# Hymba step with a mixture of experts: expert blocks of 130 to 150 rows by rank of count, and a router with stacked weights

## Chip, cores and metric

One core of one Trainium2 chip. The metric is the device time of one execution in microseconds; the time before is 1022.97 us, the median of 3 runs (1019.84 to 1026.25).

## What is computed

One layer of a streaming encoder on 1024 prompt frames and 32 frames of a running stream (1056 rows of 1024 values, float32). The first half is an mLSTM with four heads in parallel with a pooling mixer; the second half is a mixture of experts behind a router that picks one of four groups and two of its four experts:

```python
h = rmsnorm(x, norm1_g) @ w_in                       # q, k, v, o, gates, u
x = x + concat(mLSTM(q, k, v, o, gates), pool_mix(u)) @ w_out
h = rmsnorm(x, norm2_g)
pg = softmax(h @ w_rg + b_rg);  g = top-1 of pg      # group
le = (h @ w_re + b_re)[experts of g]; pv, pi = top-2 of softmax(le)
gates = pg[g] * pv / sum(pv)                         # 2 of 16 experts per row
for e in range(16):                                  # D_EXPERT = 512
    y += gates[:, e] * ((silu(h @ w_gate[e]) * (h @ w_up[e])) @ w_down[e])
return rmsnorm(x + y, norm_f_g)                      # and the states
```

Each of the 1056 rows goes to two experts: 2112 rows of expert work, 132 per expert on average.

## The kernel before, in words

Five engine programs (SyncE = SP, GpSimd = POOL, ScalarE = ACT, VectorE = DVE, TensorE = PE) are written out by hand and meet at semaphores. There are two stages.

**Main stage, about 0 to 550 us.** Nine tiles (`NT`): eight of 128 prompt rows and one of 32 rows (`DECP`, the second in order). Each engine's list of work is a loop over `i` from line 1021 (VectorE), 688 (ScalarE) and 1470 (TensorE), in which the steps of tiles i, i-1 and i-2 are interleaved. TensorE's steps are `values`, `o_and_gates`, `cols_by` (q, k, u by groups of 128 columns), `mix_start`, `mix_sums`, `pool_mix`, `out_of_pool`, `head_transposes`, `out_of_heads`, then two iterations later `router(t)` (line 1451: eight matmuls with `h2T[:, k, 0:R]` as weights and `wr[:, k, :]`, 20 columns, streamed) and `ranks(t)` (line 1461). VectorE takes the logits from PSUM in `logits(t)` (line 833), routes (`routing`, 849) and gives each (row, expert) pair a place (`places`, 879): a running count `cnt` per expert and the rank within the tile. GpSimd scatters row numbers into a list per expert in DRAM (`scatter`, 472). SP stores x1 and h2 of each tile to DRAM and loads the first expert's weights at the last tile (lines 328 to 352); among the stores of the first four tiles it fills `ye_d` with zeros.

**Expert stage.** Work is done in blocks of `BLOCK` = 150 rows of one expert. Line 1088 onward VectorE makes tables: blocks per expert, the expert and the list position of each block j (`tabi`), and signals `table_ready` (line 1116). Each engine then runs one loop `Fori(1, nblocks + 1)` whose bounds and indices it loads from `tabi`:
- SP (378): loads the weights of block j in halves when block j-1 has used them (`gu_half`, `gu_done`, `d0_used`, `dn_done`). Ahead of this loop it issues eight state stores (358 to 366), the gain nfg (373), waits for the eight stores (374) and reloads five tiles of x1 (375, 376).
- GpSimd (519): reads the block's list (`load_ids`), adds the quarter offset, gathers the rows of h2 in five indirect DMAs (`gather_tokens`, line 497).
- VectorE (1175): `products` (hid = up * silu), `gather_turn` (transposes the gathered rows, line 1131, and scales by g2, 1134, then `gx_ready`), `results` (transposes the outputs from PSUM, 1172).
- ScalarE (730): four Silus, then four stores of the block's results to `ye_d`.
- TensorE (1581): 64 matmuls gate/up (four feature groups, two halves of the contraction), then 32 for down, all over 150 columns; it waits for `gx_ready`, `w_loaded`, `y_ready` and `hid_ready`.

`first_turn` (1120) is the turn of block 1, of which the first expert is always number 0. Lines 1146 to 1160 work out, from expert, base and place, at which row of `ye_d` each result lies (`yslot`).

**Tail.** GpSimd gathers each row's two results by `yslot` (543 to 551). VectorE adds them to x1 with their gates: `sooner(t)` for the earlier result (five before `results(nblocks)`, four after it, lines 1217 to 1223), `later(t)` for the other; then final norms and stores.

A helper records the matmuls, so nearly all of them have line 1235.

## Time and profile before

| | us |
|---|---|
| median of 3 runs | 1022.97 |
| the profiled execution | 1020.06 |
| its span in the profile | 1018.4 |
| mean granted TensorE clock | 0.954 of 2.4 GHz |
| TensorE busy | 917.6 (90%) |
| VectorE busy | 430.9 (42%) |
| ScalarE busy | 161.5 (16%) |
| GpSimd busy | 211.5 (21%) |

The span runs from the first to the last instruction of the profiled execution. Its time is 1.66 us more, which lies around the span. The engines are PE (matmul), PEld (its weight loads), DVE (VectorE), ACT (ScalarE), POOL (GpSimd) and SP. In the timeline a line merges neighbouring instructions of one kind: its first number is the start, its second the length up to the end of the last one. A float32 matmul has two records in the profile, so "x64" are 32 matmuls. Ends of matmuls are modelled; intervals between starts are the better measure.

### The profile page before, as it was taken

To read this page: it belongs to the slowest core of one execution; us is meant where nothing else is said; L and a number is where in the kernel's file an instruction comes from. 1 tells how busy PE (TensorE), PEld (TensorE's weight loads), DVE (VectorE), ACT (ScalarE), POOL (GpSimd) and SP (SyncE) were. 2 spreads that over 40 slices of the span, in tenths; PEclk is the share of its full clock that TensorE was granted. 3 is DMA by queue.
4 is the path that set the end of the run, shared out by engine and by line. 5 is a ranking of instruction groups with operands and counts; after the bars stand their busy time and mean duration, and the time that the engine had idled before them with its cause. 6 is when DMAs were issued, how large, how long until landed. Compare 5 with 4: busy or idle time off the path is not lost. (4 is left out here: it accounts for less than half of the span.)

```text
span 1018.4 us, 16537 instructions
## 1 busy us (share of the span) xinstructions
PE 917.6 (90%) x6391; PEld 803.0 (79%) x6391; DVE 430.9 (42%) x1174; ACT 161.5 (16%) x456; POOL 211.5 (21%) x301
## 2 busy tenths in 40 slices
PE   6979999999999999999983779999999999999910
PEld 3964878869596886959652779999999999999910
DVE  2242364636536353552667322222222222333278
ACT  2121212121312212121221000011010101000013
POOL 1040030300303021030302322222222222222260
PEclk9989999999999999999996789999999999999965
DMA  9960706151100101010071898888888888888666
GB/s 336 309 217 1 238 2 177 31 183 56 63 1 1 63 1 42 1 42 1 1 290 49 70 381 321 300 304 310 315 309 315 311 298 297 303 308 311 247 210 236
DMA packets 91903, 184.52 MB, mean 181 GB/s; under 512 B 12933, under 2 KB 59589, under 8 KB 83666
## 3 DMA queue, kind: packets, MB, share of 16 engines
q1 hardware_dynamic: 72930, 154.86, 43.8%
q0 software_dynamic: 7328, 19.22, 6.3%
q10 hardware_dynamic: 11600, 9.84, 2.9%
q8 instruction: 28, 0.46, 0.2%
q14 instruction: 17, 0.14, 0.1%
HBM read 142.56 MB, written 41.31 MB: 181 GB/s over the span
## 5 line engine op out<-in xcount | busy, mean ns | idle before, releaser
L1235 PE MATMUL bank<-wout,win 128*128 128x150 f32 x2048 | 269.5, 294 | 21.6 <-DVE wout L1126 16.0
L1235 PEld LDWEIGHTS bank<-wout,win 128*128 128x128 f32 x2048 | 267.4, 192 | 22.2 <-issue 16.1
L1235 PE MATMUL bank<-hT,win 128*128 128x128 f32 (+1 forms) x1536 | 182.2, 280 | 0.0
L1235 PEld LDWEIGHTS bank<-hT,win 128*128 128x128 f32 x1536 | 179.3, 193 | 0.3
L1235 PE MATMUL bank<-win 128*128 128x150 f32 x1024 | 133.6, 290 | 0.0
L1235 PEld LDWEIGHTS bank<-win 128*128 128x128 f32 x1024 | 132.0, 189 | 0.0
L1235 PE MATMUL bank<-win,hT 128*128 128x260 f32 (+3 forms) x512 | 123.3, 420 | 5.0 <-DVE hT L787 3.1
L1165 DVE TENSOR_TENSOR win<-bank,win 128x150 f32<-128x150 f32 x64 | 20.0, 314 | 252.0 <-ACT win L734 252.0
L1235 PE MATMUL bank<-wout,mixT 128*128 128x512 f32 (+1 forms) x384 | 117.2, 487 | 1.8 <-ACT mixT L672 1.7
L1235 PEld LDWEIGHTS bank<-win,hT 128*128 128x128 f32 (+1 forms) x512 | 77.6, 174 | 46.5 <-issue 33.9
L1235 PEld LDWEIGHTS bank<-wout,mixT 128*128 128x128 f32 (+1 forms) x384 | 51.0, 163 | 57.8 <-issue 55.1
L497 POOL DMA_INDIRECT wout<-h_d,win x80 | 77.0, 963 | 24.6 <-issue 24.3
L507 POOL TENSOR_TENSOR win<-win,qcol 128x5 int32<-128x5 int32 x16 | 3.1, 192 | 250.7 <-DVE wout L1134 245.6
L734 ACT ACT_TABLE_LOAD x16 | 20.5, 1283 | 209.3 <-issue 197.2
L469 POOL TENSOR_SCALAR_AFFINE_SELECT dexp<-dexp 128x512 f32<-128x512 f32 (+1 forms) x9 | 5.4, 600 | 210.0 <-DVE dexp L831 210.0
L734 ACT ACTIVATE win<-bank 128x150 f32<-128x150 f32 x64 | 18.9, 297 | 168.4 <-PE bank L1235 168.4
L1172 DVE STREAM_TRANSPOSE wout<-bank 128x480 f32<-128x480 f32 (+1 forms) x48 | 29.9, 625 | 31.9 <-PE bank L1235 20.7
L1131 DVE STREAM_TRANSPOSE wout<-wout 128x1280 f32<-128x1280 f32 x15 | 37.4, 2491 | 1.8 <-DMA wout<-h_d,win 1.8
L447 POOL COPY ulast<-ubuf 128x60 f32<-128x60 f32 x7 | 3.4, 481 | 135.8 <-ACT ubuf L651 133.9
L814 DVE RECIPROCAL sig<-sig 128x512 f32<-128x512 f32 x8 | 26.8, 3352 | 0.3
L533 POOL DMA_INDIRECT win<-ye_d,yslot x18 | 23.7, 1317 | 9.4 <-issue 4.9
L476 POOL DMA_INDIRECT ids_d<-tokid,slots x18 | 18.1, 1006 | 35.4 <-DVE slots L889 30.6
(262 smaller groups left out, 774.0 us busy)
## 6 DMA issues: line engine op xcount, KB each, us to landing
win<-in_w_gate SPq DMA_DIRECT2D x32, 1024.0 KB, 5.1
win<-in_w_up SPq DMA_DIRECT2D x32, 1024.0 KB
win<-in_w_down SPq DMA_DIRECT2D x32, 1024.0 KB, 8.8
ye_d<-zeros SPq DMA_DIRECT2D x4, 4352.0 KB, 17.3
ye_d<-wout ACTq DMA_DIRECT2D x64, 150.0 KB
win<-in_w_in SPq DMA_DIRECT2D x4, 2048.0 KB, 19.5
xbuf<-in_x_prompt SPq DMA_DIRECT2D x8, 512.0 KB, 3.9
wout<-in_w_out SPq DMA_DIRECT2D x1, 4096.0 KB, 14.8
```

What stands on the lines that cost most here:

```text
L447: link(g.tensor_copy(ulast[:, 0], cur[:, :, R:R + HIST]))
L469: g.affine_select(out=dexp[0:R, :, 0:R], in_=dexp[0:R, :, 0:R], compare_op=ALU.is_ge, fill=0.0, base=0, pattern=[[0, H], [1, R]], channel_ ...
L476: g.indirect_dma_start(out=ids_d, out_offset=bass.IndirectOffsetOnAxis(ap=slots[0:R, n, t:t + 1].bitcast(U32), axis=0), in_=tokid[0:R, TIL ...
L497: g.indirect_dma_start(out=xg[:, c, :], out_offset=None, in_=h2_q, in_offset=bass.IndirectOffsetOnAxis(ap=idt[:, c:c + 1].bitcast(U32), ax ...
L507: g.tensor_tensor(idt, idraw, qcol[:, :].broadcast_to([P, NP]), ALU.add).then_inc(carried, 1)
L533: g.indirect_dma_start(out=dst[0:R, :], out_offset=None, in_=ye_d, in_offset=bass.IndirectOffsetOnAxis(ap=yslot[0:R, n, t:t + 1].bitcast(U ...
L734: a.activation(sgl[:, f % 2, :], B[GB[f]][:, 0:BLOCK], ACT.Silu).then_inc(silu_ready, 1)
L814: link(v.reciprocal(sig[0:R, b, :], sig[0:R, b, :]))
L1131: v.transpose(xgT.rearrange("p k a i -> p a k i"), xg.rearrange("p a (i k) -> p a k i", k=KD)).then_inc(xt_raw, 1)
L1165: v.tensor_tensor(hid[:, f, :], B[GB[f]][:, BLOCK:2 * BLOCK], sgl[:, f % 2, :], ALU.mult).then_inc(hid_ready, 1)
L1172: v.transpose(yrow[:, :, 32 * m0:32 * m1].rearrange("p a (m i) -> p m a i", i=32), y_window(b, m1 - m0)).then_inc(y_ready, 1)
L1235: return nc.tensor.matmul(out, lhsT, rhs, start=first, stop=last)
```

## The change

1. Blocks are taken in order of the experts' counts (expert 0 first), and the first 14 blocks have fixed sizes by rank: 150, six of 130, three of 135, two of 140, two of 145. The last two experts have 150. Rows of an expert beyond its slot go to further blocks of 150 in a general loop behind. TensorE, ScalarE and VectorE have one loop per size, and TensorE waits for the tables only ahead of the general loop. The tables become two parts: ranks and sizes (before `first_turn`), and the tables per block (behind it, with `table_ready` at their end). The slot arithmetic moves behind the first block's products and turn.
2. SP no longer loads nfg, waits for its stores and reloads x1 ahead of the weight loop; it does so behind it. The combines of the first results start with the four tiles that are still in `xbuf`.
3. The router streams h2T (128 columns) through stacked weights of 32 columns, four contraction groups in four column groups of TensorE; VectorE copies the 128 x 128 partial sums to SBUF and a second matmul with a 0/1 matrix `stk` adds and transposes them.

```diff
-    NB = NE + (2 * TOK - NE) // BLOCK
+    SLOTS = ((30, 1), (26, 6), (27, 3), (28, 2), (29, 2))
+    NS = sum(n for _, n in SLOTS)
+    SIZES = [NP * r for r, n in SLOTS for _ in range(n)] + [BLOCK] * (NE - NS)
+    YBASE = [sum(SIZES[:p]) for p in range(NE + 1)]
+    NB = 2 * NE + 1
-    YROWS = -(-NB * BLOCK // P) * P
+    YROWS = -(-(YBASE[NE] + (NB - NE) * BLOCK) // P) * P
...
@@ SP, ahead of and behind the weight loop
-            sp.dma_start(nfg, norm_f_g...).then_inc(back, 16)
-            after(sp, "stores", 16 * 8)
-            for t in range(NT - 4):
-                sp.dma_start(xa[t][0:ROWS[t], :], x1_d[...]).then_inc(back, 16)
             with sp.Fori(2, nblocks + 1) as j:
...
+            after(sp, "stores", 16 * 8)
+            for t in range(NT - 4):
+                sp.dma_start(xa[t][0:ROWS[t], :], x1_d[...]).then_inc(back, 16)
+            sp.dma_start(nfg, norm_f_g...).then_inc(back, 16)
@@ GpSimd, set-up and tail
+            link(g.memset(wr[:, :, NR:32], 0.0))
+            link(g.memset(stk[:, :], 0.0))
+            for q in range(4):
+                link(g.affine_select(out=stk[:, :], ..., base=-32 * q, pattern=[[-1, NR]], channel_multiplier=1))
+        SOONER = list(range(NT - 4, NT)) + list(range(NT - 4))
-            for t in range(NT):
-                if t >= RING:
-                    pool.wait_ge(mixed_a, t - RING + 1)
-                gather_rows(0, t, ya[t % RING], a_rows[t % RING])
+            for i, t in enumerate(SOONER):
+                if i >= RING:
+                    pool.wait_ge(mixed_a, i - RING + 1)
+                gather_rows(0, t, ya[i % RING], a_rows[i % RING])
@@ ScalarE (TensorE and VectorE alike)
-            with act.Fori(1, nblocks + 1) as j:
+            j0 = 1
+            for r, count in SLOTS:
+                with act.Fori(j0, j0 + count) as j:
+                    expert(j, r, j * (NP * r) + (YBASE[j0 - 1] - NP * r * j0))
+                j0 += count
+            with act.Fori(NS + 1, nblocks + 1) as j:
+                expert(j, RP, j * BLOCK + (YBASE[NS] - BLOCK * (NS + 1)))
@@ VectorE, router
+            def partial_logits(t):
+                R = ROWS[t]
+                after(dve, "lo_done", t + 1)
+                v.tensor_copy(lgT[:, 0:R], B[7][:, 0:R]).then_inc(S["lgT_ready"], 1)
             def logits(t):
-                after(dve, "lo_done", t + 1)
-                v.scalar_tensor_tensor(out=rt[0:R, 0:NR], in0=B[7][0:R, 0:NR], ...)
+                after(dve, "lg_done", t + 1)
+                v.scalar_tensor_tensor(out=rt[0:R, 0:NR], in0=B[7][0:R, P:P + NR], ...)
@@ VectorE, tables: ahead of first_turn
+            link(v.scalar_tensor_tensor(out=key, in0=cnt[:, :], scalar=float(NE), in1=iof[:, 0:NE], ...))
+            link(v.memset(key[:, 0:1], -1.0))
+            link(v.tensor_tensor(cube[:, 0], across(key), wide(key, [P, NE, NE]), ALU.is_lt))
+            link(v.tensor_reduce(out=pos, in_=cube[:, 0], axis=AX.X, op=ALU.add))
...          # size and base by pos: five more passes over 16 x 16; then over, big, ext, xin, xpos
             first_turn()
+            block_tables()          # 21 operations, 8 of them over 34 x 16; table_ready at their end
+            products(1, SLOTS[0][0])
+            turn(1)
...          # yslot: 26 operations before this, now with thr, row1, row2 as well
+            results(1, SLOTS[0][0])
...          # loops over SLOTS[1:], then Fori(NS + 1, nblocks)
-            products(nblocks)
-            dve.wait_ge(back, 16 * (NT - 3))
-            for t in range(RING):
-                sooner(t)
-            results(nblocks)
-            for t in range(RING, NT):
-                sooner(t)
+            products(nblocks, RP)
+            for i in range(4):
+                sooner(i)
+            results(nblocks, RP)
+            for i in range(4, NT):     # sooner(4) waits for back
+                sooner(i)
@@ TensorE
-                    last = mm(B[7][0:R, 0:NR], h2T[:, k, 0:R], wr[:, k, :], k == 0, k == KD - 1)
+                    q = k % 4
+                    last = mm(B[7][32 * q:32 * q + 32, 0:R], wr[:, k, :], h2T[:, k, 0:R], k < 4, k >= KD - 4)
+            def router_sums(t):
+                after(pe, "lgT_ready", t + 1)
+                mm(B[7][0:R, P:P + NR], lgT[:, 0:R], stk[:, :]).then_inc(S["lg_done"], 1)
...          # order now: router(i-2), q group 0, router_sums(i-2), q group 1, mix_start(i-1), q groups 2, 3, k
-            after(pe, "table_ready", 1)
-            with pe.Fori(1, nblocks + 1) as j:
+            def expert(j, r):          # the block as before, over N = 5 * r columns
...
+            for r, count in SLOTS:
+                with pe.Fori(j0, j0 + count) as j:
+                    expert(j, r)
+                j0 += count
+            after(pe, "table_ready", 1)
+            nblocks = pe.value_load(...)
+            with pe.Fori(NS + 1, nblocks + 1) as j:
+                expert(j, RP)
```

## Rows read from the trace of the kernel before

**Rows 1.** The page's slices: busy tenths in 40 equal slices of the span

```profile
PE   6979999999999999999983779999999999999910
DMA  9960706151100101010071898888888888888666
```

**Rows 2.** Windows: us, busy (instructions) of PE, PEld, DVE, ACT, POOL; clock, DMA share, GB/s

```profile
300.00:400.00 100.00, 100.00 (x581) 75.14 (x581) 53.53 (x160) 21.67 (x66) 19.56 (x26) 1.00 0.07 27
575.00:583.00 8.00, 8.00 (x65) 8.00 (x64) 0.31 (x1) 0.30 (x1) 0.00 (x0) 1.00 1.04 48
602.00:604.00 2.00, 2.00 (x9) 2.00 (x9) 0.00 (x0) 0.00 (x0) 0.00 (x0) 0.50 1.04 418
742.23:766.74 24.51, 24.51 (x195) 24.51 (x193) 7.04 (x9) 2.47 (x5) 5.94 (x8) 1.00 0.87 309
```

**Rows 3.** Timeline of TensorE within prompt tiles: start, length, instruction

```profile
307.08 7.31 PE L1235 MATMUL bank<-hT,win 128*128 128x128 f32 x64
314.23 7.03 PE L1235 MATMUL bank<-wout,mixT 128*128 128x512 f32 x16
...
344.25 1.86 PE L1235 MATMUL bank<-wr,h2T 128*128 128x20 f32 x16
345.95 2.03 PE L1235 MATMUL bank<-hT,win 128*128 128x128 f32 x16
```

**Rows 4.** Timeline of TensorE: half of w_out for the 32-row tile

```profile
147.23 1.95 PE L1235 MATMUL bank<-wout,mixT 128*32 128x128 f32 x64
```

**Rows 5.** Timeline of VectorE within a prompt tile

```profile
348.18 0.29 DVE L821 COPY hmt<-bank 128x128 f32<-128x128 f32 x1 [1.72 <-PE bank L1331]
```

**Rows 6.** Timeline, end of the main stage

```profile
539.88 1.96 PE L1235 MATMUL bank<-wr,h2T 128*128 128x20 f32 x16 [1.50 <-DVE h2T L796]
...
541.88 0.24 DVE L837 SCALAR_TENSOR_TENSOR rt<-bank,sm,brt 128x20 f32<-128x20 f32 x1 [0.24 <-PE bank L1235]
```

**Rows 7.** Timeline: VectorE's tables, the first gathered piece, TensorE's first block

```profile
552.47 0.65 DVE L1104 TENSOR_TENSOR dexp<-kw,iof 1x480 f32<-1x480 f32 x1
...
557.30 0.14 DVE L1116 CAST tabi<-kw 1x1 int32<-1x1 f32 x1
...
559.91 0.64 DVE L1123 STREAM_TRANSPOSE wout<-wout 128x256 f32<-128x256 f32 x1 [2.47 <-DMA wout<-h_d,win]
...
567.32 7.96 PE L1235 MATMUL bank<-wout,win 128*128 128x150 f32 x39 [16.03 <-DVE wout L1126]
```

**Rows 8.** The chain that ended last: start, us, what

```profile
568.94 16.29 DMA out<-xn
...
588.96 12.69 DMA win<-in_w_up
601.69 361.43 PE bank L1235 x2808
```

**Rows 9.** Timeline: last gather issue for block 2, and its turn

```profile
573.13 0.94 POOL L497 DMA_INDIRECT wout<-h_d,win  x1 [0.30 <-issue]
...
589.06 2.51 DVE L1131 STREAM_TRANSPOSE wout<-wout 128x1280 f32<-128x1280 f32 x1 [1.75 <-DMA wout<-h_d,win]
591.60 1.49 DVE L1134 TENSOR_TENSOR wout<-wout,g2m 128x1280 f32<-128x1280 f32 x1
```

**Rows 10.** Timeline of TensorE: one block, from its down stage to the next

```profile
742.23 8.35 PE L1235 MATMUL bank<-win 128*128 128x150 f32 x64
750.42 16.48 PE L1235 MATMUL bank<-wout,win 128*128 128x150 f32 x128
766.74 8.35 PE L1235 MATMUL bank<-win 128*128 128x150 f32 x64
```

**Rows 11.** DMA issues: line's tensors, queue, count, KB each, median us to landing

```profile
win<-ids_d POOLq DMA_DIRECT2D x16, 2.5 KB, 5.8
```

**Rows 12.** Timeline of VectorE: tail

```profile
971.85 1.63 DVE L1172 STREAM_TRANSPOSE wout<-bank 128x480 f32<-128x480 f32 x3
...
986.73 3.24 DVE L1187 SCALAR_TENSOR_TENSOR xn<-win,gateo,xn 128x256 f32<-128x256 f32 x8 [4.86 <-DMA win<-ye_d,yslot]
```

More of the change, by code:

```diff
@@ L109, in hymba_step @@
         Cs = sb("Cs", [P, H, V1])
[L110 removed]
+        wr = sb("wr", [P, KD, 32])
+        stk = sb("stk", [P, NR])
+        lgT = sb("lgT", [P, P])
         poolw = sb("poolw", [P, NG, GW])
@@ L1017, in _ @@
             link(v.tensor_scalar(ecap[:, :], iof[:, 0:NE], float(CAP), None, ALU.mult))
+            p0 = 0
+            for r, count in SLOTS + ((RP, NE - NS),):
+                n = NP * r
+                v.memset(szv[:, 0, p0:p0 + count], float(n))
+                v.tensor_scalar(szv[:, 1, p0:p0 + count], iof[:, p0:p0 + count], float(n), float(YBASE[p0] - n * p0),
+                                ALU.mult, ALU.add)
+                p0 += count
             for n in range(NG):
@@ L1116, in _, with across @@
-            v.tensor_copy(tabi[:, 2 * NJ:2 * NJ + 1], ci[:, NE - 1:NE]).then_inc(S["table_ready"], 1)
-            dve.wait_ge(S["table_ready"], 1)
+            key, pos, size, base, over, ext, xin, xpos, thr, row1, row2, val = (vec[:, c, :] for c in range(12))
+            def across(x):
+                return x.unsqueeze(1).broadcast_to([P, NE, NE])
+            link(v.scalar_tensor_tensor(out=key, in0=cnt[:, :], scalar=float(NE), in1=iof[:, 0:NE], op0=ALU.mult, op1=ALU.add))
+            link(v.memset(key[:, 0:1], -1.0))
@@ new lines, in _ @@
+            link(v.tensor_reduce(out=base, in_=cube[:, 1], axis=AX.X, op=ALU.add))
+            link(v.tensor_scalar(rt[:, 0:MAXB], iof[:, 0:MAXB], float(BLOCK), None, ALU.mult))
+            link(v.tensor_tensor(over, cnt[:, :], size, ALU.subtract))
+            link(v.tensor_tensor(big, wide(over, [P, NE, MAXB]), rt[:, 0:MAXB].unsqueeze(1).broadcast_to([P, NE, MAXB]), ALU.is_gt))
+            link(v.tensor_reduce(out=ext, in_=big, axis=AX.X, op=ALU.add))
+            link(v.tensor_tensor_scan(xin, ones[:, 0:NE], ext, 0.0, ALU.mult, ALU.add))
@@ new lines, in results, with turn @@
+            def results(j, r):
+                dve.wait_ge(y_stored, 16 * NQ * j)
+                for n, (b, m0, m1) in enumerate(YB):
+                    dve.wait_ge(dn_done, 3 * j + (n + 1))
+                    v.transpose(yrow[:, :, 32 * m0:32 * m1].rearrange("p a (m i) -> p m a i", i=32),
+                                y_window(b, m1 - m0, r)).then_inc(y_ready, 1)
+            def turn(j):
+                dve.wait_ge(gu_done, 4 * j + 4)
+                gather_turn(j)
+            block_tables()
@@ L1189, in combine, with sooner @@
                 last.then_inc(done, 1)
-            def sooner(t):
-                dve.wait_ge(a_rows[t % RING], 16 * (t // RING + 1))
-                combine(0, ya[t % RING], t, mixed_a)
+            def sooner(i):
+                if i == 4:
+                    dve.wait_ge(back, 16 * (NT - 3))
+                dve.wait_ge(a_rows[i % RING], 16 * (i // RING + 1))
+                combine(0, ya[i % RING], SOONER[i], mixed_a)
             def later(t):
                 dve.wait_ge(b_rows[t], 16)
-                dve.wait_ge(mixed_a, t + 1)
+                dve.wait_ge(mixed_a, NT)
                 combine(1, yb[t], t, mixed)
```

173 lines of the change are left out of this document (105 added, 68 removed).

## Prediction

> **What bounds the kernel now.** I read the page's slices first [rows 1]: TensorE is at 9 tenths nearly everywhere, with one dip in the middle (the routing tables and the first gathered block) and a tail without it; the DMA row is busy at the start, low through the first half, and at 8 tenths through the expert half. The windows sharpen this [rows 2]: 300 to 400 us has TensorE busy for all 100 us at granted clock 1.00 with the DMA at 0.07, and one expert block (742.23 to 766.74) has TensorE busy throughout, DMA share 0.87, 309 GB/s. So both halves are bound by TensorE, and the expert half has about 13% of the DMA time in reserve. The timeline of one prompt tile [rows 3] gives intervals between matmul starts: 32 matmuls over 128 columns take 314.23 - 307.08 = 7.15 us, 223.4 ns each; the eight router matmuls, which stream only 20 columns, take 1.70 us, 212.5 ns each. In the expert blocks [rows 10] two successive down stages start 24.51 us apart, and a block has 64 + 32 = 96 matmuls over 150 columns: 255.3 ns each, 250.0 ns of it for 600 column passes at 2.4 GHz and 5.3 ns over. The chain that ended last [rows 8] shows what stands between block 1 and block 2: the small state stores (16.29 us after their last issue), then weights (12.69 us), then 361.43 us of TensorE alone.
>
> **Router (six full tiles).** The 1.70 us of a tile's eight matmuls become eight over 128 columns with 32 weight columns in four different output groups. Rows of that shape exist: w_out for the 32-row tile issues 32 such matmuls in 1.95 us, 61 ns each [rows 4]. Eight: 0.49 us; the added sum is one 20-column matmul, 0.21 us. Saving 1.70 - 0.70 = 1.0 us. Bounds: no concurrency (8 x 223 + 212 ns, 0.3 us lost) to 1.1 us saved. I take 1.0, the row of the same shape. VectorE pays a 128x128 copy, 0.29 us, inside waits: the row that gives this price stands right behind the logits and waits 1.72 us for TensorE itself [rows 5]. The sum waits for that copy behind one query group, 8 x 0.223 = 1.8 us, longer than the copy and two hand-overs; queued behind it on TensorE is the second query group, and if the cover went it would cost a few tenths. Router reads of tiles 0 and 2 to 6 lie in the fully busy stretch: -6.0 us. The 32-row tile: 0.
>
> At the end of the main stage VectorE leads. Tile 7's copy stands between numerators and head_out, on the way to the head transposes; if they wait for VectorE there, as I take it, +0.3, else 0. Tile 8's router runs in a serial chain: before, from 539.88 to VectorE's logits at 541.88; now 0.5 of matmuls, then the copy, which starts only once VectorE is through with the norm (541.88 less the 0.24 it waited: 541.64), 0.3, then the sum and a hand-over, some 0.5 to 0.6: logits at about 542.7, +0.8 [rows 6]. Sum of the router: **-4.9** (from -6.5 to +1).
>
> The added set-up (seven short GpSimd instructions, ten VectorE ones) lies in the first slice, where the DMA is at 9 and TensorE at 6 tenths, waiting for weights [rows 1]; the larger zero fill (4 x 4864 instead of 4352 KB) lies in a stage with DMA share 0.07 [rows 2]. Both 0; uncovered, the fill would cost 2.1 MB at 400 GB/s, 5 us.
>
> **Tables and block 1.** The tables start some 1.9 us ahead of the 552.47 row [rows 7], at 550.6. Before first_turn now stand seventeen operations, seven of them over 256 elements. The 480-element row is 0.65 us [rows 7], so about 0.43 each; with the small ones and gaps 5.3 us: done at 555.9, before the first gathered piece is there at 559.91. Cost 0, block 1 still starts at 567.3, released by first_turn [rows 7]. The block tables (eight passes over 34 x 16 = 544 elements at 0.72, thirteen small ones at 0.17, gaps) take 8.7 us behind first_turn: table_ready at 575.9 instead of 557.4 [rows 7]. TensorE doesn't need it. SP, GpSimd and ScalarE do, and three things queue behind it:
> - SP's eight stores are issued from 575.9 to 579.8. They drained 16.3 us after the last issue before [rows 8]; same again: 596.1. The windows show how such a stretch looks: 575 to 583 has share 1.04 at only 48 GB/s [rows 2]. The wait for the stores and the five reloads of x1 (2.2 MB) are gone from ahead of block 2's weights, which are issued at about 580.6. If they queue behind the stores: 596.1 + 2 MB at 418 GB/s (5 us) + 2 us for the last of the 16 engines = 603. If they don't, they land before 596.
> - GpSimd's index list: issued at 577, 5.8 us [rows 11], then five gathers to 589.5. Before, the last gather was issued at 574.1 and VectorE had it at 589.06, 3.8 us after the stores had drained [rows 8, 9]. Same distance: 599.9; the turn (2.51 + 1.49 us) ends at 603.9. With the full 15 us after the last issue: 608.5.
> - ScalarE's first Silu follows the third quarter of the gate/up stage, at 580 or later: covered by 4 us.
> I take 603.5 for the start of block 2. Before it was 601.69 with 8 of its records already done (14 x 192 + 128 = 2816, the row has 2808 [rows 8]), 1.3 us at the lower clock, so 600.4. **+3.1** (from -4.4 to +8.1). TensorE ends block 1 after 24.5 us and some 3 of slow clock, at about 595, so it idles 8 to 9 us, and the clock will be at 0.50, 1.2 GHz, for some us as in 602 to 604 [rows 2]; that loss (about 3 us) is in both.
>
> The Trainium skill (DMA: Bandwidth & Descriptors, "Two DMAs through the same engine are not ordered") says that the descriptors of one queue of one DMA engine start in order. By it the weights queue behind the stores, which is what the 603 supposes; without it the start would be that of the gather.
>
> Slot arithmetic (some 8 us more than before) moves behind turn(1): results(1) ends about 10.6 us after turn(1), and TensorE's down stage needs it 14 us after: covered by 3.7 us.
>
> **Blocks 2 to 16.** From the reference's routing of its own inputs I counted the rows per expert: expert 0 has 146, the others 107, 119, 124, 125, 125, 126, 127, 129, 133, 133, 140, 140, 144, 146, 148. Every one fits its slot (130 x6, 135 x3, 140 x2, 145 x2, 150 x2), one exactly (140 in 140). The trace agrees as far as it can: 16 blocks of 150. So still 16 blocks. Per matmul: N/0.6 ns + 5.3; at 130 that gives 222.0, but 128 columns already take 223.4 [rows 3], so 224. Times 96: 21.50, 22.11, 22.91, 23.71, 24.51 us. Sum of the 15: 129.0 + 66.3 + 45.8 + 47.4 + 49.0 = 337.5, against 367.6: **-30.1**. Can the rest keep up? A block moves 24.51 x 309 = 7.57 MB; at 21.50 us less 80 KB of stores that is 348 GB/s, and the 21.3 us of DMA work become a share of 0.97 to 0.99. The engines have done 418 GB/s at 1.04 [rows 2]. Weights are issued two thirds of a block ahead (about 14 us against 5 us of transfer), so small lags don't reach TensorE. VectorE's turn ends 4.9 us after the gate/up stage, the down stage lasts 7.2: covered by 2.3 us (3.4 now).
>
> **Tail.** Four combines instead of five before the last results. The transposes start only at 971.85 behind the fifth, a combine is 1.6 us, and TensorE is through at 963.12 + 32 x 0.2553 = 971.3 [rows 8, 12]. Now the first two are done from 970.3 on, the last waits for TensorE and ends at 972.2 instead of 973.5: **-1.3**; the stores, the second gathers (waited for until 986.73 [rows 12]) and the end follow. The one more combine behind results lies in that wait. The reloads of x1 now come behind the last weights, some 20 us before use: 0.
>
> **Sum:** -4.9 + 3.1 - 30.1 - 1.3 = -33.2. The profiled execution took 1020.06 (span 1018.4, 1.66 around it), so 986.9. The runs' median, 1022.97, is 0.29% above it; by the same ratio 989.7 us. A measurement here tells about 1% from no change.
>
> **Rivals.**
> 1. The DMA becomes the bound at 130 and 135 rows. For: 0.97 to 0.99 leaves nothing, and gathers and stores come in small pieces. Against: shares of 1.0 and above over whole windows. If no more than 0.93 is kept up, a block needs 21.3/0.93 = 22.9 us: 6 x 1.4 + 3 x 0.8 = 10.8 lost: 1000.5.
> 2. The plan of slots fails: rounding moves one token and an expert overflows its slot, so a seventeenth block of 150 runs. Only if both experts with 140 gain one. +24.5: 1014.
> 3. Each new loop body costs a wait for its code. TensorE, VectorE and ScalarE now have six or seven bodies instead of one. If a first pass over a body waits once for a small load in the busy queues, 5.8 us [rows 11], five of them take 29 us: 1019, no gain. Slower side: if jumps back wait too, 15 passages x 5.8 = 87 us: 1077. It decides from 33.2/15 = 2.2 us per passage. Against: the one body of now jumps back 15 times with no gap (the down stage's 32 matmuls end where the next block starts) [rows 10], and each new body has the same length.
> The Trainium skill (Runtime: NRT & Kernel Launch, "Instruction fetch mechanics") warns of this: a taken branch to a target outside the two pages held forces a fetch before the engine goes on. The trace of before doesn't contradict it, as its one body may fit.
>
> **Chances.** Forecast 0.75 (alone 978 to 998: the hop's ends, -7.5 and +5.0 about its value, and the router's, some -4 and +3 without their extremes); rival 1 0.12; rival 2 0.04; rival 3 0.05 for entries only, 0.04 for slower. Range 978 to 1003 holds the first two. Faster by over 1% (below 1012.7): 0.87; within 1%: rival 2 and the half of rival 3, 0.09; slower: 0.04.
>
> **What would show it.** Right: router groups of 0.5 us per tile; a tile's period 1.0 us shorter; block periods of 21.5, 22.1, 22.9, 23.7, 24.5 us with the DMA share near 0.98 in the first six; SP's stores issued about 8.7 us after first_turn; block 2 starting some 36 us after block 1. Wrong: waits for w_gate or w_up within the 130-row blocks (rival 1), a seventeenth group of Silus (rival 2), gaps at the first pass of a body with no releaser but issue (rival 3), or TensorE idle at head transposes in the main stage, which would mean that VectorE's chain, not TensorE, set the tile's period.

## The result, and the profile after

The changed kernel is slower: 1054.45 us, the median of 4 runs (1053.48 to 1055.86), against 1022.72 for the kernel before in the same session (1019.84 to 1026.25). The ratio is 1.031, with a 95% interval from 1.0275 to 1.0345, so the kernel got slower where it had been forecast to get faster. The profiled execution took 1053.8 us, with a span of 1052.2. The forecast was 989.7 us in a range up to 1003. The slices of the page of after, which answer to [rows 1]:

```profile
PE 887.6 (84%) x6409; PEld 766.4 (73%) x6409; DVE 442.8 (42%) x1231; ACT 140.9 (13%) x441; POOL 209.7 (20%) x307
...
PE   6979999999999999999835489999999999583910
...
PEclk9989999999999999999966889999999999786965
DMA  9960707070101010000714969988888888543676
```

TensorE does less work than before (887.6 us against 917.6), so the narrower blocks are there. But the row of TensorE has two dips that it had not: a deeper one in the middle (3, 5, 4) and a new one near the end (5, 8, 3), where the clock and the DMA row fall as well. TensorE's timeline shows both, with start, length, count of records and the idle time ahead:

```profile
563.17 19.10 PE L1332 MATMUL bank<-wout,win 128*128 128x150 f32 x128 [18.20 <-DVE wout L1197]
...
609.80 15.94 PE L1332 MATMUL bank<-wout,win 128*128 128x130 f32 x128 [19.25 <-DVE wout L1205]
...
633.28 5.23 PE L1332 MATMUL bank<-wout,win 128*128 128x130 f32 x44
639.27 9.63 PE L1332 MATMUL bank<-wout,win 128*128 128x130 f32 x84 [0.76 <-issue]
...
883.73 8.05 PE L1332 MATMUL bank<-win 128*128 128x145 f32 x64
891.62 15.95 PE L1332 MATMUL bank<-wout,win 128*128 128x145 f32 x128
924.39 10.96 PE L1332 MATMUL bank<-win 128*128 128x145 f32 x64 [16.82 <-DVE win L1220]
...
968.60 11.32 PE L1332 MATMUL bank<-win 128*128 128x150 f32 x64 [16.93 <-DVE win L1220]
...
996.08 8.35 PE L1332 MATMUL bank<-win 128*128 128x150 f32 x64
```

Three things are to be seen. Block 2 starts at 609.80, 46.6 us after block 1, where it was 33.1 before. Where the rows of [rows 10] ran without a gap, the gate/up stages of blocks 3 to 13 stand still for 0.5 to 1.4 us in the middle. The profile names "issue" as the releaser, that is, it shows nothing that TensorE waited for. These are called the pauses below. And the down stages of blocks 14 and 15 wait 17 us each for `products`. TensorE is idle there from about 908 us on, its granted clock is 0.50 (1.2 GHz) from 912 to 924 us, and the down stage behind takes 10.96 us in place of 8.05. The cause of these two waits is one engine back, in ScalarE's timeline:

```profile
868.12 3.94 ACTq L762 DMA_DIRECT2D ye_d<-wout  x4
...
892.52 30.55 ACTq L762 DMA_DIRECT2D ye_d<-wout  x4
923.49 0.47 ACT L758 ACTIVATE win<-bank 128x145 f32<-128x145 f32 x2 [39.27 <-issue]
...
937.78 29.53 ACTq L762 DMA_DIRECT2D ye_d<-wout  x4
967.68 0.48 ACT L758 ACTIVATE win<-bank 128x150 f32<-128x150 f32 x2 [42.96 <-issue]
```

The four stores of a block's results occupy ScalarE for some 4 us, except behind the two blocks of 145 rows, where they take 30. The next block's Silus stand behind them in ScalarE's program. The chain that ended last goes the same way (start, us, what):

```profile
893.42 5.90 ACTq L762
899.48 17.18 ACTq L762
916.81 18.12 DMA ye_d<-wout
```

The whole difference, from starts in the two traces (33.7 us between the profiled executions, with the terms of the forecast beside them):

| stretch | measured | forecast |
|---|---|---|
| start of block 1: 563.17 against 567.32 [rows 7] | -4.15 | -4.9 |
| from block 1 to block 2: 46.6 against 33.1 | +13.5 | +3.1 |
| block 2 to the end of block 16: 394.6 against 370.7 | +23.9 | -30.1 |
| tail: 47.8 against 47.3 | +0.5 | -1.3 |

### The profile page after: what moved, and what is told of

The parts are those of the page before. It is cut to its first block and busy times, and to the rows that moved or that the text cites. A ratio compares the mean times of both kernels' runs of the same rounds, so it can differ in the third digit from the quotient of the medians.

```text
span 1052.2 us, 16614 instructions
## 1 busy us (share of the span) xinstructions
PE 887.6 (84%) x6409; PEld 766.4 (73%) x6409; DVE 442.8 (42%) x1231; ACT 140.9 (13%) x441; POOL 209.7 (20%) x307
## 5 line engine op out<-in xcount | busy, mean ns | idle before, releaser
L1332 PE MATMUL bank<-wout,win 128*128 128x130 f32 (+4 forms) x2048 | 252.0, 283 | 48.5 <-DVE wout L1205 19.3
L1332 PEld LDWEIGHTS bank<-wout,win 128*128 128x128 f32 x2048 | 247.0, 192 | 52.2 <-issue 33.6
L1332 PE MATMUL bank<-win 128*128 128x130 f32 (+4 forms) x1024 | 129.2, 288 | 34.0 <-DVE win L1220 34.0
L1332 PEld LDWEIGHTS bank<-win 128*128 128x128 f32 x1024 | 127.4, 196 | 34.7 <-DVE win L1220 34.7
L1220 DVE TENSOR_TENSOR win<-bank,win 128x130 f32<-128x130 f32 (+4 forms) x64 | 18.7, 301 | 259.6 <-ACT win L758 256.4
L758 ACT ACTIVATE win<-bank 128x130 f32<-128x130 f32 (+4 forms) x64 | 17.7, 285 | 404.9 <-PE bank L1332 280.8
L1205 DVE TENSOR_TENSOR wout<-wout,g2m 128x1280 f32<-128x1280 f32 x15 | 22.4, 1493 | 0.5
L798 DVE TENSOR_SCALAR sm<-sm 128x1 f32<-128x1 f32 (+3 forms) x27 | 5.2, 194 | 38.0 <-ACT sm L588 38.0
```

The lines of the kernel that those rows point to most:

```text
L758: a.activation(sgl[:, f % 2, 0:n], B[GB[f]][:, 0:n], ACT.Silu).then_inc(silu_ready, 1)
L1205: v.tensor_tensor(flat, flat, wide(g2m[:, :], [P, KD, NP * 32]), ALU.mult).then_inc(gx_ready, 1)
L1220: v.tensor_tensor(hid[:, f, 0:n], B[GB[f]][:, n:2 * n], sgl[:, f % 2, 0:n], ALU.mult).then_inc(hid_ready, 1)
L1332: return nc.tensor.matmul(out, lhsT, rhs, start=first, stop=last)
```

## The experiments

Two theories stood at the start. A: the stores of 29 partitions are the main loss. C: block 2 is late because of the state stores. The pauses had none yet. Ratios are against runs of the kernel before beside them. Where no ratio is given, the kernel ran once; such a kernel leaves out rows or needs more blocks, and only its trace is of use.

**No blocks of 145 rows.**

```diff
-    SLOTS = ((30, 1), (26, 6), (27, 3), (28, 2), (29, 2))
+    SLOTS = ((30, 1), (26, 6), (27, 3), (28, 2))
```

> Theory A (the stores of 29 partitions hold ScalarE's queue for 30 us in blocks 14 and 15, whose four result stores took 30.55 and 29.53 us against 4 us for the other sizes): with two blocks of 150 rows in place of the two of 145, all result stores take 3.9 to 4.4 us, the block periods there fall from 40.66 and 44.21 to about 24.6 us, the clock does not fall to 0.50 in blocks 15 and 16, and the time is 1053.8 - 16.1 - 19.6 - 3 = about 1015 us (1012 to 1018). Rival (the transfers that follow the loop, or the amount of data, hold the queue, not the shape): the long stores stay in the same two blocks, and the time stays within 5 us of 1053.

1018.35 us, ratio 0.9947 (0.9931 to 0.9962), 0.35 us above the range given. The stores take 4.09 to 4.27 us behind every one of the last four blocks.

**145 rows computed, 30 partitions stored.**

```diff
-                rows = ye_d[bass.ds(base, n), :].rearrange("(i a) d -> i a d", a=NP)
+                s = 30 if r == 29 else r
+                rows = ye_d[bass.ds(base, NP * s), :].rearrange("(i a) d -> i a d", a=NP)
-                    act.dma_start(rows[...], yrow[32 * q:32 * q + r, :, :])
+                    act.dma_start(rows[...], yrow[32 * q:32 * q + s, :, :])
...          # YBASE, szv and base step by NP * 30 for these two
```

> The two blocks of 145 rows are computed as before, but each of their stores takes 30 partitions to rows of ye_d of their own (the last five hold values that nothing reads). Theory A, in the narrow form that it is the 29 partitions and not the 145 columns: the stores fall to 4 us and the time is that of no29 less 2 x 0.7 us, 1011 to 1017 us. Rival (something else in blocks of 145 rows, as the Silus or the transposes): the long waits stay, about 1053 us.

1017.29 us, ratio 0.995 (0.9931 to 0.9969), 0.3 us above the range given. Storing more bytes took 37.2 us off the changed kernel, so neither the bytes nor the 145 columns are the cause. With this alone it is a little faster than before.

**The same shape in the kernel before.**

```diff
-                rows = ye_d[bass.ds(j * BLOCK - BLOCK, BLOCK), :]...
+                rows = ye_d[bass.ds(j * BLOCK - BLOCK, 29 * NP), :]...
-                    act.dma_start(rows[...], yrow[32 * q:32 * q + RP, :, :])
+                    act.dma_start(rows[...], yrow[32 * q:32 * q + 29, :, :])
```

> The kernel before with every block's result stores cut to 29 of 30 partitions (five rows of each block are not stored; nothing else differs). Theory A: each block's four stores take some 30 us of issue on ScalarE instead of 4, more than the 24.5 us of a block, so that all 16 blocks are paced by ScalarE at some 40 to 44 us: 1020 + 15 x 16 to 20 = 1260 to 1320 us, with TensorE's clock at 0.5 in part of each. Rival (29 partitions are harmless in themselves, the cost came from the changed kernel's loops or rows): 1020 us, within 3.

This kernel leaves five rows of each block unstored. 1343.9 us, above the range: a block takes 44.7 us (686.03 - 641.30), as TensorE's timeline shows.

```profile
641.30 10.91 PE L1235 MATMUL bank<-win 128*128 128x150 f32 x64 [18.81 <-DVE win L1165]
...
686.03 10.74 PE L1235 MATMUL bank<-win 128*128 128x150 f32 x64 [17.50 <-DVE win L1165]
```

One partition fewer in a store, 321 us more in the kernel. The change's loops and tables have no part in it.

**A map of partition counts.** The changed kernel, every block at 150 rows, with the count of partitions stored set per block. The rows beyond it are left out.

```diff
-    SLOTS = ((30, 1), (26, 6), (27, 3), (28, 2), (29, 2))
+    SLOTS = ((30, 1),) * 14
+    STORE = (30, 32, 31, 29, 28, 27, 26, 25, 24, 23, 22, 21, 20, 19)
...
+                    act.dma_start(rows[...], yrow[32 * q:32 * q + STORE[j0 - 1], :, :])
```

> The changed kernel with all blocks at 150 rows, where the result stores of blocks 1 to 14 take 30, 32, 31, 29, 28, 27, 26, 25, 24, 23, 22, 21, 20 and 19 partitions (rows beyond are not stored). Theory A1 (a count of partitions that is prime beyond 16 cannot be cut evenly, and all its pieces go one way): about 30 us of issue for 31, 29, 23 and 19, about 4 us for the others. Theory A2 (it is 29 alone, or counts just under a limit): only 29, or 29 and 31. Theory A3 (the largest divisor up to 16 decides): 31, 29, 23, 19 have 1 (30 us), 26 and 22 have 13 and 11, 25 has 5, which then takes some 5 to 8 us, between the two.

ScalarE's queue in its timeline, with 31, 29 and 28 partitions, then 25, 23 and 19:

```profile
663.78 32.10 ACTq L763 DMA_DIRECT2D ye_d<-wout  x4
713.50 26.19 ACTq L763 DMA_DIRECT2D ye_d<-wout  x4
754.92 3.58 ACTq L763 DMA_DIRECT2D ye_d<-wout  x4
...
825.62 3.96 ACTq L763 DMA_DIRECT2D ye_d<-wout  x4
...
874.63 26.95 ACTq L763 DMA_DIRECT2D ye_d<-wout  x4
...
986.79 23.85 ACTq L763 DMA_DIRECT2D ye_d<-wout  x4
```

31, 29, 23 and 19 partitions take 24 to 32 us; 32, 30, 28, 27, 26, 25, 24, 22, 21 and 20 take 3.2 to 4.3. A1 holds, and A3's finer step for 25 is not there (3.96 us). The Trainium skill (DMA: Bandwidth & Descriptors, "Why a DMA increments its semaphore by 16 and not by 1") has a rule that fits: a DMA goes to the largest number of engines up to 16 that divides the slowest dimension on both sides. By it a store of 29 partitions goes to one DMA engine and one of 28 to fourteen. The map agrees, and so does the wait of block 14 in the changed kernel: from 918 to 924 us nothing but ScalarE's queue (q10) moves data, at a DMA share of 0.07, which is 1.1 of the 16 engines.

```profile
918.00:924.00 6.00, 0.00 (x0) 0.00 (x0) 0.19 (x1) 0.47 (x2) 0.00 (x0) 0.50 0.07 24
```

```profile
q10 hardware_dynamic: 143, 0.15, 6.8%
```

Why ScalarE itself stands still while one engine works off its stores was not tried.

**State stores behind block 2's weights**, on top of the padded kernel.

```diff
-            for st, Co, no in (...):   # and the six further lines of the eight state stores
+            loads(2)
+            for st, Co, no in (...):   # the eight state stores
-            with sp.Fori(2, nblocks + 1) as j:
+            with sp.Fori(3, nblocks + 1) as j:
```

> pad30 with the eight state stores issued behind the six weight loads of block 2 instead of ahead of them. Theory C (the start of block 2 is late because its list of rows waits 19 us, and its weights some 12 us, behind the state stores with their pieces of 4 bytes): the list lands some 3 to 6 us after its issue, block 2 starts within 24 to 30 us of block 1 instead of 46.6, and the time is 14 to 22 us less than pad30: 990 to 1002 us. Rival (the list waits for the tables and for VectorE, not for the stores): the gathers of block 2 move by less than 3 us, and the time is within 4 us of pad30. A third way: the stores then delay block 3's list and weights by as much, and the gain is given back there.

1006.15 us, ratio 0.9842 (0.9804 to 0.9879), 11.1 us less than the padded kernel where 14 to 22 were expected. The index list of block 2 in GpSimd's timeline, in the changed kernel and then here: `add_quarter` (TENSOR_TENSOR) needs the list.

```profile
574.20 0.75 POOL L524 DMA_DIRECT2D win<-ids_d  x1 [15.28 <-issue]
593.71 0.19 POOL L528 TENSOR_TENSOR win<-win,qcol 128x5 int32<-128x5 int32 x1 [18.76 <-DMA win<-ids_d]
```

```profile
574.13 0.76 POOL L528 DMA_DIRECT2D win<-ids_d  x1 [14.87 <-issue]
577.87 0.19 POOL L532 TENSOR_TENSOR win<-win,qcol 128x5 int32<-128x5 int32 x1 [2.98 <-DMA win<-ids_d]
```

GpSimd waits 18.8 us for a list of 2.5 KB behind the state stores, and 3.0 without them. Block 2 starts at 594.82 and not at 609.80: 15 us. But block 3 starts only 10 us earlier, and not by the third way, as it waits for neither list nor weights. TensorE stands still within block 2:

```profile
594.82 8.50 PE L1339 MATMUL bank<-wout,win 128*128 128x130 f32 x59 [4.04 <-DVE wout L1212]
604.82 2.62 PE L1339 MATMUL bank<-wout,win 128*128 128x130 f32 x22 [1.50 <-issue]
...
609.47 0.27 PE L1339 MATMUL bank<-wout,win 128*128 128x130 f32 x1 [1.56 <-issue]
```

That makes 3.4 us of idle time without a wait of the program, in the first pass of TensorE's 130-row loop and while the state stores are in the queues.

**TensorE's loops written out.** All kernels with the chain of widths had the pauses so far.

```diff
             for r, count in SLOTS:
-                with pe.Fori(j0, j0 + count) as j:
+                for j in range(j0, j0 + count):
                     expert(j, r)
```

> stores_behind with TensorE's fourteen fixed blocks written out one behind the other in place of five loops (nothing else differs). In stores_behind each gate/up stage at 130 rows stands still for about 1.3 us, some 5.3 us after its start, with no wait of the program at that place. Theory B1 (the pause belongs to the jump back of the loop, and comes 45 records behind it): without jumps the pauses vanish, and the time falls by 8 to 14 us, to 992 to 998 us. Rival B2 (the pause comes from what the other engines or the DMA queues do at that time: the result stores end and the gathers begin there): the pauses stay at the same 5.3 us, and the time is within 3 us of stores_behind's 1006. Rival B3 (straight code has to be fetched as well, and the pauses come at other places, as often): pauses of the same sum spread over the blocks, time within 5 us of 1006.

992.46 us, ratio 0.9726 (0.9709 to 0.9743): B1's number. The pauses are gone, but for 2.8 us in blocks 2 and 3.

```profile
644.60 14.46 PE L1339 MATMUL bank<-wout,win 128*128 128x130 f32 x128
...
666.04 14.46 PE L1339 MATMUL bank<-wout,win 128*128 128x130 f32 x128
```

The period is 666.04 - 644.60 = 21.44 us; 21.50 had been forecast.

**Two blocks per pass.**

```diff
+                    with pe.Fori(j0, j0 + count // 2 * 2, 2) as j:
+                        expert(j, r)
+                        expert(j + 1, r)
```

> stores_behind with two blocks per pass in TensorE's loops where the count allows it, so 7 jumps fewer (the six blocks of 130 rows in three passes). B1: the pause appears in the first block of each pass alone, and the second has none; the time is 4 to 7 us less than stores_behind, 999 to 1002 us. B2: every block of 130 rows keeps its pause, 1006 us. B3: a pause in every block, the second one's at another place.

993.86 us, ratio 0.9738 (0.9696 to 0.9779). B1 in its own words misses: from block 3 on no block keeps a pause, where every first one should. Block 2 keeps 3.9 us of idle time with "issue" as the releaser. A jump back alone does not make the pause.

**All fourteen sizes at 150 rows.**

```diff
-    SLOTS = ((30, 1), (26, 6), (27, 3), (28, 2), (29, 2))
+    SLOTS = ((30, 1), (30, 6), (30, 3), (30, 2), (30, 2))
```

> The changed kernel with all fourteen sizes set to 150 rows, loops, tables, tail and router as changed. By the recorded trace of the changed kernel: block 2 starts 46 us after block 1 in place of 33, the blocks take 24.5 us, and the time is 1020.1 - 4.1 (router) + 13 (block 2) + 0.6 (tail) = about 1029.5 us (1026 to 1033). B1 with cover (the pause behind a jump is hidden while TensorE runs 150 columns): no pause, 1029. Were the pause a matter of the several loops, each block would have one here too, some 14 us more, 1043.

1031.55 us, ratio 1.0103 (1.0086 to 1.012), in the range given, with no pauses in blocks 2 and later: the change without its narrow blocks loses 10 us, which is the late block 2 less what the router gives.

**130 rows in the kernel before, in one loop and in several.**

```diff
-    NP, RP, NQ = 5, 30, 4
+    NP, RP, NQ = 5, 26, 4
...          # NB = 31, which these inputs' 24 blocks fit; for the others also:
-            with pe.Fori(1, nblocks + 1) as j:
+            with pe.Fori(1, 2) as j: ...       # (1, 2), (2, 8), (8, 11), (11, 13), (13, 15), (15, nblocks + 1)
+            with pe.Fori(1, 13) as j: ...      # or (1, 13), (13, nblocks + 1)
```

> The kernel before, its single loop kept, with blocks of 130 rows in place of 150: the 16 experts then need 24 blocks. Theory B1 (short blocks of one per jump, wherever the loop comes from): each gate/up stage shows the pause of 0.8 to 1.4 us some 5.3 us after its start, the block period is about 23 us, and the time 1020 + 22 x 23.0 - 14 x 24.5 + (two stages) = about 1180 us. Rival (the pause comes from the changed kernel's chain of loops or its code layout): no pause, period 21.5 us, about 1145 us.

> b_rows130 (one loop of 130 rows in the kernel before: no pause, 1146.6 us) with TensorE's loop cut into six loops of the same body over blocks 1, 2 to 7, 8 to 10, 11 and 12, 13 and 14, and the rest. Theory B4 (the pause belongs to loops that have other code behind them, where the columns are too few to cover it): a pause of 0.8 to 1.4 us in the blocks of the loops ahead of the last, none in the last one's, 1158 to 1165 us. Rival B5 (it came from other engines' changed loops at the same time): no pause, 1147 us but for the first pass of each loop.

> b_rows130 with TensorE's loop cut in two, over blocks 1 to 12 and over the rest. B4: pauses in blocks 3 to 12, none in the last loop, 1155 to 1160 us. If it takes more code than one more body of a loop: no pause here, though in b_rows130_five. B5: no pause in either.

1146.63, 1147.16 and 1144.0 us: no pause in any from block 2 on, and periods of 21.45 us. Neither narrow blocks, nor jumps, nor a chain of loops on TensorE is enough. (The second cut TensorE's loop into six.)

**The changed kernel with equal widths.**

```diff
-    SLOTS = ((30, 1), (26, 6), (27, 3), (28, 2), (29, 2))
+    SLOTS = ((30, 1), (26, 13))                              # one_loop130
+    SLOTS = ((30, 1), (26, 6), (26, 3), (26, 2), (26, 2))    # chain130
```

> stores_behind with the sizes 150 once and 130 thirteen times, so one loop of 130 rows on each engine (experts with more rows take further blocks of 150 in the general loop; the total time is not the point). Theory B6 (the pause needs a chain of loops of 130 on the engines besides TensorE, or several bodies in TensorE's code): no pause, block period 21.5 us. Rival B7 (the pause needs only the changed kernel's place in the code, with one loop too): a pause of 0.7 to 1.4 us in blocks 4 to 14, period 22.7 to 23.3 us, as in stores_behind.

> one_loop130 with the thirteen blocks of 130 rows in loops of 6, 3, 2 and 2, all of the same width. B6: pauses as in stores_behind, in every loop but the last of the chain perhaps, 13 x 1.3 = 17 us more than one_loop130. B7: the same as one_loop130, within 3 us. Neither has a pause in its blocks of 150 rows.

1103.62 and 1099.05 us, more blocks being needed; no pause in either past block 2. Both theories miss: chain130's loop of six has the same instructions as in the kernel with state stores behind, and differs from it only in the widths of what follows.

**The chain of widths without the disturbed start.** This is the last kernel of this section (stores_spread, below) with TensorE's loops put back.

```diff
-                for j in range(j0, j0 + count):
+                with pe.Fori(j0, j0 + count) as j:
```

> stores_spread with TensorE's five loops put back in place of the fourteen blocks written out. Theory B8 (the pauses come with the chain of loops whose widths differ, whatever goes before): pauses of 0.5 to 1.4 us in the blocks of 130 to 145 rows, and 11 to 15 us more than stores_spread, 992 to 996 us. Rival B9 (the pauses are a rhythm into which blocks 1 to 3 put the engines in the changed kernel, with its late block 2 or 3, and which keeps itself up): no pauses here, 980 to 983 us.

994.58 us, ratio 0.9743 (0.9726 to 0.976), against 980.71 with the loops written out. The pauses are back in blocks 2 to 11, though not in 12 to 14:

```profile
635.32 5.33 PE L1365 MATMUL bank<-wout,win 128*128 128x130 f32 x45
642.00 9.43 PE L1365 MATMUL bank<-wout,win 128*128 128x130 f32 x83 [1.35 <-issue]
```

B8 holds in the main: the pauses come with the chain of loops of several widths, whatever the start is like. Between the two pairs of kernels that differ in TensorE's loops alone lie 13.7 and 13.9 us.

**The router alone**, in the kernel before.

```diff
+                    last = mm(B[7][32 * q:32 * q + 32, 0:R], wr[:, k, :], h2T[:, k, 0:R], k < 4, k >= KD - 4)
...          # with router_sums, partial_logits, stk and wr of 32 columns, as in the change
```

> The kernel before with the new router alone. By the trace of the changed kernel TensorE's last main-stage matmul comes 6.3 us earlier, and the first block 4.15 us; here the first block starts 563.2 us or some tenths later in place of 567.3, and the time falls by 4 us to about 1018.5. Rival 1 (the weights of block 1, issued earlier by less than that, hold the start): less than 2 us. Rival 2 (block 2 waits for what SP issues and not for block 1, so that the gain is lost there): block 2 still starts near 600, and the time is within 1 us of before's.

1014.14 us, ratio 0.9932 (0.9918 to 0.9945): 7.1 us, where 4 had been expected and the prediction's bounds ended at 6.5. The first block starts at 560.91, 6.4 us earlier, and block 2's 120 records behind the wait for w_up at 595.20 against 601.69 [rows 8], so SP's stores moved along.

**Block 2's expert and list worked out first.**

```diff
+            link(v.tensor_scalar(row1[0:1], pos[0:1], 1.0, None, ALU.is_equal))
+            link(v.tensor_tensor(row1[0:1], row1[0:1], iof[0:1, 0:NE], ALU.mult))
+            link(v.tensor_reduce(out=row2[0:1, 0:1], in_=row1[0:1], axis=AX.X, op=ALU.add))
+            link(v.tensor_scalar(row2[0:1, 1:2], row2[0:1, 0:1], float(CAP), None, ALU.mult))
+            v.tensor_copy(row2i[:, :], row2[0:1, 0:2]).then_inc(S["second_ready"], 1)
...          # GpSimd and SP take block 2 from row2i, and from block 3 on the tables
```

> pe_straight where VectorE works out the expert of block 2 and its place in the list ahead of first_turn (five small operations, about 1 us, while it waits for the gathered rows), and GpSimd and SP take block 2 from these two numbers instead of from the full tables. In pe_straight block 2 started 4.16 us after TensorE had ended block 1, released by VectorE's turn, which hung from list, gathers and tables. Theory C: list and gathers now run during the first block, the turn of block 2 ends before block 1 does, the 4.16 us go, and the time is 987 to 990 us. Rival: the gathers of block 2 or the earlier weights delay block 1 (its turn or its own loads), or the weights of block 2 are late next: 991 to 995 us.

992.36 us, as with TensorE's loops written out: the rival. Block 2 now follows block 1 without a gap, and block 3 waits:

```profile
590.85 14.45 PE L1351 MATMUL bank<-wout,win 128*128 128x130 f32 x128
...
619.99 2.07 PE L1351 MATMUL bank<-wout,win 128*128 128x130 f32 x8 [7.54 <-DMA win<-in_w_gate]
623.66 15.28 PE L1351 MATMUL bank<-wout,win 128*128 128x130 f32 x120 [1.61 <-DMA win<-in_w_up]
```

**State stores behind all weights.** The eight stores move to just ahead of the reload of x1.

```diff
             with sp.Fori(3, nblocks + 1) as j:
                 loads(j)
+            for st, Co, no in (...):   # the eight state stores
             after(sp, "stores", 16 * 8)
```

> second_first with the eight state stores moved behind the whole weight loop, just ahead of the reload of x1. In second_first block 2 followed block 1 without a gap, but block 3 waited 7.54 us for w_gate and 1.61 us for w_up, whose loads had been queued behind the state stores. Theory C: these waits go, block 3 starts some 21.5 us after block 2 and not 28, and the time is 992.4 less 7 to 9 = 983 to 986 us. Rival: the stores, some 25 us long, now meet the last blocks' weights or the reloads of x1 and delay the tail: 988 us or more.

990.44 us, ratio 0.9706 (0.9687 to 0.9725): the rival again. TensorE had no gap from 564.20 on and ended at 928.4, but the tail took 60.4 us. The stores' price had moved from block 3 to the last gathers.

**State stores one by one.**

```diff
+            for j in range(3, NS + 1):
+                loads(j)
+                if j >= NS - 7:
+                    state_store(j - (NS - 7))
+            with sp.Fori(NS + 1, nblocks + 1) as j:
+                loads(j)
```

> second_first with SP's first fourteen passes written out and one of the eight state stores behind the weights of each of blocks 7 to 14 (two of them some 10 us long). In stores_last TensorE's blocks ran without a gap to 928.4 us, 10 us before second_first's, but the tail took 60.4 us in place of 50, because the state stores were in the queues when the last blocks' results had to be stored and gathered. Theory C: spread out, each store fits beside the weights of a block; TensorE ends near 929 us and the tail takes 50: 979 to 983 us. Rival: the two stores of 4-byte pieces (n_prompt, n_sample) still hold the queues for some 8 us each and delay the weights of the next block: 986 to 991 us.

980.71 us, ratio 0.9608 (0.9594 to 0.9621), in the range given. One wait of 0.53 us for w_up, at block 11, is all that TensorE shows of them. This version beats the kernel before by 40.8 us and the changed one by 73.7. Its windows of 640 to 740 us, and the same of the changed kernel (us, busy time of PE, PEld, DVE, ACT, POOL, then clock, DMA share, GB/s):

```profile
640.00:740.00 100.00, 100.00 (x893) 100.00 (x892) 33.01 (x42) 5.62 (x20) 23.96 (x33) 1.00 0.97 336
```

```profile
640.00:740.00 100.00, 95.07 (x837) 93.75 (x837) 28.42 (x39) 5.30 (x19) 23.68 (x32) 1.00 0.89 325
```

## Why the prediction was wrong

**Blocks 2 to 16: the step failed by 54.0 us (+23.9 for -30.1), and it turned the sign.** The durations behind it were right: 21.44 us per block of 130 rows where 21.50 was forecast, and with the state stores one by one and TensorE's code straight, blocks 2 to 16 take 929.35 - 591.56 = 337.8 us against the sum's 337.5. What failed is the sentence "Can the rest keep up?". It asked this of the DMA's bytes, of the weights and of VectorE, and never of ScalarE's four stores, whose shape changes with r and which stand ahead of the next Silus. Of the five counts 30, 26, 27, 28 and 29 one is prime, and padding it gave back 37.2 us. The Trainium skill had this rule, on the page that the prediction cited for another one; looked up for each `yrow[32q:32q+r]`, it would have singled out 29. The starts in the changed kernel's timeline, against those of the kernel with the state stores one by one, close the account: blocks 14 and 15 lost 39.9 us (43.56 and 44.58 us for 23.68 and 24.51), the pauses of blocks 3 to 13 lost 15.5 (258.34 us for 242.9), and block 2 lost 2.0 (23.48 us for 21.44), where it lost 3.0 before. Less those 3.0, and less 0.5 by which the durations came out shorter than forecast, that is the 54.

**Rival 3 came nearest to the pauses and priced them too high.** It asked for 2.2 us per passage before the sign turns; the pauses made eleven blocks 0.7 to 1.9 us longer, from start to start. Its text, a wait at the first pass of a body or at the jump, is not what they are either: such a pause comes 5.1 to 5.5 us into a block of the changed kernel, on later passes as on first ones, and not in chains of one width. The Trainium skill's page (Runtime: NRT & Kernel Launch, "Instruction fetch mechanics") would put such a pause down to a fetch behind a taken branch. The traces don't bear that out for these pauses. The changed kernel's page has 36 packets of queue q8 (instructions) and not 28 as before, for five more loop bodies on TensorE, and not one or two more per pass. The kernel with the loops 130, 130, 130 and 130 has 36 as well, and no such pause. And between 700 and 750 us of the changed kernel, where two pauses lie, q8 moves nothing.

```profile
q8 instruction: 36, 0.59, 0.2%
```

What the pause is stays open. Shown is when it appears, what it costs, and that straight code or two blocks per pass removes it. What rival 3 describes may lie behind the idle time in block 2 of the kernel with the state stores behind: that is a first pass, and the packet of q8 that starts there at 603 us takes 2.3 us, where the next one, at 621 us, takes 0.96. That TensorE waits for it was not tried.

**Tables and block 2: +13.5 in place of +3.1.** The place was right and block 2 was released by the turn of its gathered rows, as the sum supposed. The tables took 8.6 us behind first_turn (563.03 to 571.60; 8.7 forecast) and SP's stores went out at 571.63. The mis-sized term is the list: 5.8 us [rows 11] is the median over all blocks, and this one was issued with the eight state stores in the queues:

```profile
571.64 0.52 POOLq L539
...
574.20 19.36 DMA win<-ids_d
```

It lands at 593.6, and only then can five gathers be issued (6 us) and land (6 us); the sum had let them wait in the queues beside the stores, at before's distance from their end. Before, the tables came first, and GpSimd fetched the list of block 2 two us ahead of SP's first state store:

```profile
563.06 0.75 POOL L503 DMA_DIRECT2D win<-ids_d  x1
```

```profile
565.03 0.39 SPq L359 DMA_DIRECT2D out<-Cp  x1
```

That was the hidden gain of the old order, and the move of the tables behind first_turn gave it up.

**Router: -4.9 forecast, -4.15 in place, -6.4 alone.** The rows that answer to [rows 3]:

```profile
339.54 0.64 PE L1332 MATMUL bank<-h2T,wr 128*32 128x128 f32 x16
340.12 2.05 PE L1332 MATMUL bank<-hT,win 128*128 128x128 f32 x16
342.01 0.30 PE L1332 MATMUL bank<-stk,lgT 128*128 128x20 f32 x2
342.15 2.03 PE L1332 MATMUL bank<-hT,win 128*128 128x128 f32 x16
```

The eight matmuls take 0.58 us (0.49 forecast) and the added one 0.14. A tile's period fell from 60.10 (404.35 - 344.25) to 59.32 us (398.86 - 339.54), 0.8 and not 1.0; but the losses put down for tiles 7 and 8 (+1.1) did not come, and TensorE ended the main stage 6.3 us earlier. That -4.15 lies near -4.9 is luck: the changed kernel loses 2 us of this again between the last scatter of rows and block 1's list (4.8 us between the two issues, 2.75 with the router alone); why was not tried.

**Tail: -1.3 forecast, +0.5 measured,** and 1.3 more than before in the padded kernel (48.6 us). The forecast started from a TensorE end of 971.3; by the last down stage (962.79, 8.35 us long) it was 971.1. The reloads of x1 behind the weight loop had been costed at nothing, "some 20 us before use". In SP's timeline they go out together with block 15's results (980.66 in ScalarE's queue):

```profile
980.70 0.82 SPq L401 DMA_DIRECT2D xn<-x_d  x2
```

GpSimd's first gather of results, which waits for these stores, is issued at 994.36, 14.6 us after block 16 began (979.76); before, it was 956.10, 9.6 us after (946.47). In the padded kernel, without a slow store, it is 15.5 us (957.10 and 941.57). So the four first combines end later than the five did: 1.7 us behind TensorE (1006.09) and not 0.8 (971.92). That the reloads are what holds the stores was read from the two traces and not tried by itself.

**Rival 1** (the DMA as the bound) is out: at a share of 0.97 TensorE is busy for all of 640 to 740 us, once the pauses are gone. **Rival 2** did not happen: there are 64 Silus, 16 blocks. The range as it was worked out also took 4 us below the router's value, where the router's own bounds allowed 1.6.

## What to carry to other kernels

When a block size changes, go through every DMA whose outermost count changes with it, and factor that count: stores of 19, 23, 29 and 31 partitions, prime counts beyond 16, made a block 11 to 20 us longer here, where five rows fewer had saved 0.8 us, and one partition more of padding removed that. A small list behind a batch of stores with tiny pieces waited for the batch, so fetch first what the next block hangs on, and deal such stores out one per block. And a chain of loops of different sizes should be looked at pass by pass, as its pauses show in no wait.

## What the runs showed of the hardware that had not been expected

- Four stores by 29 partitions took 26 to 31 us of the issuing engine's time in the changed kernel and the map, four by 28 or 30 partitions 4 us. 31, 23 and 19 partitions (24 to 32 us) behave like 29. While such a store alone was under way, the DMA engines were busy for 0.07 of their time, one of 16.
- Eight state stores of under 0.6 MB in all kept a list of 2.5 KB waiting for 18.8 us, and dealt out one per block they left one wait of 0.53 us.
- TensorE paused 0.5 to 1.4 us in most blocks of 130 to 145 rows when its code was a chain of loops of several widths, and, past the first blocks, not with one width (130 or 150), with two blocks per pass or with straight code. Why is open.
